# Dense gates of a product-key expert layer: both keys of eight tokens marked in one VectorE comparison, the weighing of four tokens moved to GpSimd

## The reference, cut to what matters

```python
v1, i1 = lax.top_k(s1, PEER_TOPK)
v2, i2 = lax.top_k(s2, PEER_TOPK)
...
top_s, pos = lax.top_k(cand, PEER_TOPK)
eidx = jnp.take_along_axis(cidx, pos, axis=-1)
gates = jax.nn.softmax(top_s, axis=-1)
...
act = jnp.einsum('td,ted->te', xb, u_tab[eb]).astype(jnp.float32)
act = jax.nn.gelu(act, approximate=False) * gb
return jnp.einsum('te,ted->td', act.astype(xb.dtype), v_tab[eb])
```

## Time and profile before

| what | us |
|---|---|
| median of 3 runs | 3903.03 |
| the three runs | 3894.15, 3903.03, 3905.36 |
| the profiled execution's own time | 3899.16 |
| its span, first to last instruction | 3897.4 |
| gate stage, from the first mark to the last copy out of PSUM | 118.8 |

### The profile page before, as it was taken

How to read it: one execution, slowest core, us unless ns; L and a number is a source line. 1 busy time by engine, 2 the same in 40 slices (tenths; PEclk the granted TensorE clock), 3 DMA queues, 4 the chain that set the end, 5 groups by cost and what they waited for, 6 DMA issues and landing times.

```text
span 3897.4 us, 59055 instructions
## 1 busy us (share of the span) xinstructions
PE 3546.3 (91%) x20968; PEld 3128.5 (80%) x20968; DVE 2908.0 (75%) x3762; ACT 1175.3 (30%) x1890; POOL 1160.8 (30%) x986
## 2 busy tenths in 40 slices
PE   7999999999997896994879999999999999999886
PEld 3687787778776683443779999999999999999885
DVE  1555565664665312799879999999999999999987
ACT  1222212322222222113933333333333333333331
POOL 1343444444441544002022222222222222222231
PEclk8999999999998897997989999999999999999998
DMA  9443333333334432112689999999999999999995
GB/s 362 152 128 112 108 119 116 110 116 116 114 111 152 166 111 90 65 65 71 207 310 373 374 366 369 367 371 374 369 367 374 374 368 377 370 362 374 352 350 222
DMA packets 300858, 950.05 MB, mean 244 GB/s; under 512 B 24386, under 2 KB 67842, under 8 KB 230018
## 3 DMA queue, kind: packets, MB, share of 16 engines
q1 hardware_dynamic: 243202, 542.47, 40.1%
q0 software_dynamic: 55296, 402.68, 26.4%
q10 hardware_dynamic: 2304, 4.20, 0.3%
HBM read 914.55 MB, written 33.60 MB: 243 GB/s over the span
## 4 chain that ended last, share of the span: by engine, by line
DVE 16%; DVEq 15%; PE 6%; issue 6%; ACT 4%; DMA 3%; ACTq 0%; SPq 0%; POOLq 0%
DVEq L1987 14%; DVE Ub L1985 6%; ACT UH L1209 3%; DVE acc_r L1993 2%; DVE UL L1213 2%; DMA VR<-peer_v 2%; DVE VL L1949 2%; DVE acc_x L1993 1%; PE PS L1834 1%; PE PS L1835 1%; PE PS L1836 1%; DVE GB L1955 1%; ACT AHa L1896 1%; PE PS L1227 0%; PE PS L1228 0%
## 5 line engine op out<-in xcount | busy, mean ns | idle before, releaser
L1227 PE MATMUL PS<-xh,UH 128*128 128x320 f32 x2048 | 633.3, 309 | 17.6 <-POOL UL L1213 17.6
L1835 PE MATMUL PS<-AL,VH 128*128 128x320 f32 x2048 | 641.4, 313 | 0.0
L1228 PE MATMUL PS<-xl,UH 128*128 128x320 f32 x2048 | 633.6, 309 | 0.0
L1229 PE MATMUL PS<-xh,UL 128*128 128x320 f32 x2048 | 633.4, 309 | 0.0
L375 PE MATMUL PS<-hH,WH 128*128 128x512 f32 (+1 forms) x1312 | 484.0, 369 | 8.3 <-ACT kk L690 7.4
L1787 POOL DMA_INDIRECT Vb<-peer_v,stage x192 | 242.8, 1264 | 772.8 <-DVE acc_r L1993 513.1
L376 PE MATMUL PS<-hL,WH 128*128 128x512 f32 (+1 forms) x1312 | 464.0, 354 | 0.0
L377 PE MATMUL PS<-hH,WL 128*128 128x512 f32 (+1 forms) x1312 | 463.1, 353 | 0.0
L1834 PE MATMUL PS<-AHa,VH 128*128 128x320 f32 x1024 | 325.6, 318 | 110.3 <-DVE AL L1959 81.7
L1227 PEld LDWEIGHTS PS<-xh,UH 128*128 128x128 f32 x2048 | 385.2, 188 | 17.8 <-issue 17.8
L1787 POOL DMA_INDIRECT Ub<-peer_u,stage x192 | 225.3, 1174 | 583.4 <-DVE Ub L1985 535.7
(11 more groups left out here) (331 smaller groups left out, 7284.8 us busy)
## 6 DMA issues: line engine op xcount, KB each, us to landing
UR<-peer_ut SPq DMA_DIRECT2D x128, 1024.0 KB, 7.0
VR<-peer_v SPq DMA_DIRECT2D x256, 512.0 KB, 8.0
AW<-wada SPq DMA_DIRECT2D x128, 512.0 KB, 3.8
WR<-wseq SPq DMA_DIRECT2D x224, 256.0 KB, 2.6
wr<-wada SPq DMA_DIRECT2D x32, 1024.0 KB, 11.3
gates_dram<-GS SPq DMA_DIRECT2D x10, 2048.0 KB, 8.9
GB<-gates_dram SPq DMA_DIRECT2D x32, 640.0 KB, 6.4
oR<-wout SPq DMA_DIRECT2D x32, 512.0 KB, 3.8
```

Of the source, the lines that this page charges most:

```text
L1227: pe.matmul(dst, UH[:, j % 2, k, :], xh[:, k, :], start=(k == 0), stop=False)
L1228: pe.matmul(dst, UH[:, j % 2, k, :], xl[:, k, :], start=False, stop=False)
L1229: last = pe.matmul(dst, UL[:, j % 2, k, :], xh[:, k, :], start=False, stop=(k == KT - 1))
L1835: pe.matmul(low, VH[:, slot, j, cols], AL[:, :, b, :], start=False, stop=False)
```

## The change

- `GACT` goes from 6 to 4: ScalarE weighs the last four tokens of a unit, no longer six.
- `W1` and `O2` become two halves of one buffer `marked`, so that VectorE marks the first and the second keys of all eight tokens in one comparison of 128x2048, with one semaphore behind it. The two instructions that compared and weighed in one are gone.
- GpSimd, after `u_low` of the first four blocks, weighs the first four tokens of each unit in place: four `tensor_scalar` multiplications of 128x128, after waiting for the mark. TensorE waits for these in place of `s_w1`. The fifth `u_low` stands behind all 160 of them in GpSimd's order.

(A short description that came with the change speaks of three tokens on GpSimd and five on ScalarE; the diff sets four and four, and that is what is built.)

```diff
-GACT = 6
+GACT = 4
...
-            O2 = over("O2", "lng", [P, GSLOTS, GU, P], skip=ROW // 2)
-            W1 = over("W1", "lng", [P, GSLOTS, GU, P], skip=ROW // 2 + 2 * ROW)
+            marked = over("marked", "lng", [P, GSLOTS, 2, GU, P], skip=ROW // 2)
+            W1, O2 = marked[:, :, 0, :, :], marked[:, :, 1, :, :]
...
-                            pe.wait_ge(s_w1, 8 * r + j + 1)
+                            pe.wait_ge(s_wp, 8 * r + j + 1)
...
-                    for j in range(SUPER + 1):
-                        u_low(pool, j // SUPER, j % SUPER)
+                    for j in range(SUPER):
+                        u_low(pool, 0, j)
+                    for n in range(GUNITS):
+                        pool.wait_ge(s_e1, n + 1)
+                        pool.sem_inc(s_passed)
+                        for i in range(GU - GACT):
+                            w = W1[:, n % GSLOTS, i, :]
+                            last = pool.tensor_scalar(w, w, pairT[:, 2, GU * n + i:GU * n + i + 1], None, ALU.mult)
+                        last.then_inc(s_wp, 1)
+                    u_low(pool, 1, 0)
...
-                            dve.tensor_tensor(W1[:, slot, GU - GACT:GU, :],
-                                              pairT[:, 0, bass.ds(t0 + GU - GACT, GACT)].unsqueeze(2).to_broadcast([P, GACT, P]),
-                                              iota.unsqueeze(1).to_broadcast([P, GACT, P]), ALU.is_equal).then_inc(s_e1, 1)
-                            dve.tensor_tensor(O2[:, slot, :, :], pairT[:, 1, bass.ds(t0, GU)].unsqueeze(2).to_broadcast([P, GU, P]),
-                                              iota.unsqueeze(1).to_broadcast([P, GU, P]), ALU.is_equal)
-                            for i in range(GU - GACT):
-                                tok = bass.ds(t0 + i, 1)
-                                last = dve.tensor_scalar(W1[:, slot, i, :], iota, pairT[:, 0, tok], pairT[:, 2, tok], ALU.is_equal, ALU.mult)
-                            last.then_inc(s_w1, 1)
+                            dve.tensor_tensor(marked[:, slot, :, :, :], pairT[:, 0:2, bass.ds(t0, GU)].unsqueeze(3).to_broadcast([P, 2, GU, P]),
+                                              iota.unsqueeze(1).unsqueeze(1).to_broadcast([P, 2, GU, P]), ALU.is_equal).then_inc(s_e1, 1)
```

More of the change, by code:

```diff
@@ L1169, in program @@
         s_pairs, s_prpe, s_prev = sem("pairs_ready"), sem("pairs_turned"), sem("pairs_turned_kept")
-        s_e1, s_w1, s_wa1 = sem("first_keys_marked"), sem("keys_marked_and_weighted"), sem("first_keys_weighted_act")
+        s_e1, s_wp, s_wa1 = sem("keys_marked"), sem("first_keys_weighted_pool"), sem("first_keys_weighted_act")
         s_gpe, s_gev = sem("gate_tokens_summed"), sem("gate_tokens_kept")
```

## The result

The changed kernel takes 3962.8 us (median of four runs, 3960.95 to 3967.31), against 3900.6 of before on the same chips (with a fourth run beside the three of the table ahead): ratio 1.0159, 95% interval 1.0145 to 1.0172. It is **62 us slower**, three and a half times the 18 us that were forecast, and outside the range. The direction and the mechanism were those of the forecast; the price of a weighing was not.

What follows compares the result with a forecast made beforehand. ScalarE was taken to bound the gate stage (118.8 us) at 2.66 us a unit. With the change 40 x 3.23 = 129.2, plus 4.6, 1.0 and 2, total 137: +18 us, 3921 us, range 3904 to 3950.

Steps and rivals of the forecast that it cites:

- What bounds the kernel: Gate stage: ScalarE sets the pace at 2.66 us a unit; what the 118.8 us stage gains or loses, the kernel does.
- The exclusion: VectorE's mark and GpSimd's weighing block each other wholly, so a unit costs their sum, 3.23 us in place of 2.66.
- The rounds: Gate stage: VectorE marks up to four units ahead and stops; GpSimd then finishes units, TensorE getting about three in a bunch.
- I take 0.27 us for each of four in a row, near the select: Price of GpSimd's weighing of 128x128, taken from the select's row: 1.08 us a unit for four.
- 166 plus little: Rival of dearer weighings: 0.5 us each, a unit 4.15 us, +47, 3950 us; chance 0.20 together with slow clock.
- The brief lock: Rival: GpSimd holds the port only 0.11 us a weighing, a unit costs about 2.85 us, +3 to +10; chance 0.16.
- A slow TensorE: Rival: bursts of units lower TensorE's clock, +15 us on top, 3936; chance 0.20 together with dearer weighings.
- No exclusion: Rival: marks leave GpSimd room, VectorE's 2.20 us is the gate stage's pace, -16 us, 3887; chance 0.09.
- What was costed at nothing: Fifth `u_low` (4.5 us at most if uncovered), two `dense_dots` (7 us each), stores, GpSimd's waits and instruction fetch: hidden, 0 us.

Runs made afterwards that it cites:

- the PSUM run: Changed kernel with iota copied once into PSUM, where VectorE's mark reads it; GpSimd still does four weighings a unit: 3889.8 us, ratio to before 0.9970.
- the run with 512 elements: Changed kernel with one GpSimd tensor_scalar of 128x512 per unit, by one token's gate for all four, in place of four multiplications: 3924.0 us, one run.

## Why the prediction was wrong

**What bounds the kernel, and that the stage passes on what it loses: right.** 59.0 of 62 us are the stage, and the wait behind it is unchanged.

**The exclusion: right.** It had been read from two long `u_low`; the PSUM run shows it by taking it away. The mark's share of the sum is 2.0 us, where the forecast had 2.15. The rounds were also as described: VectorE runs ahead, stops at `s_gpe`, and GpSimd then delivers three units in a bunch (two in some later rounds).

**The term that failed: "I take 0.27 us for each of four in a row, near the select".** It measures 0.58 from start to start. Put into the same sum, with 0.44 for the one behind each mark (2.59 less the mark's 2.15), a unit is 2.15 + 0.44 + 3 x 0.58 = 4.33 and 40 of them 173. The profile's 172.1 is that number only because the wait of 3.7 us and the two marks that cost GpSimd nothing nearly cancel. The error is 1.1 us in a unit, 44 us in 40 of them (the end of the stage was 3 us shorter than I had it). And the upper end that I had put on this price, 0.53 by the two-input rate, was itself too low: I had argued that an instruction with one tensor input can't be dearer than one with two. Its price per element, 2.5 ns, is above that of the subtraction's 2.1 and three times the cast's 0.83. The rows showed three kinds of GpSimd instruction and none of this one; for an operation that no row shows, rates of other operations were no bound. With its 0.5 a unit would be 4.15 and the loss some 7 us less than it was; and I had closed that case with "166 plus little", though the forecast's own sum had 8 us for the end.

**The brief lock.** I gave it 0.16, as a way to a small loss. For this instruction the hold on VectorE is indeed brief, and that saved nothing. In the run with 512 elements a mark started at 1864.64 us, 1.0 us into a multiplication of 1.56 us, and was not delayed:

```profile
L1687 DVE TENSOR_TENSOR marked<-pairT,iota x1: 2291/2291/2291, 1864.6 to 1864.6; 128x2048 f32<-128x2048 f32 x1
L1459 POOL TENSOR_SCALAR marked<-marked,pairT x3: 1558/2713/5306, 1860.9 to 1865.2; 128x512 f32<-128x512 f32 x3
```

The rows are the mark and the three multiplications around it, of which the one of 1558 ns ran from 1863.64; the last, from 1865.2 on, waited for the rest of this mark and a whole second one, 5.3 us. The next round repeats it: a mark of 2.29 us from 1874.18, 1.0 us into a multiplication of 1.56. Three units take 9.54 us there, 3.18 each, where 1.56 + 2.01 would be 3.57: for this instruction the two times do not add up wholly, though the prediction had the two engines block each other wholly. I infer that a mark is held up only by the first part of such an instruction, while the weighing behind a mark is held up for nearly all of it: in the changed kernel marks lost 0.1 us and weighings 2.0. Since GpSimd was the pace, it was its loss that counted: 4 x 0.58 + 2.0 = 4.33 again. I had asked how long GpSimd holds VectorE up; the question was which of the two engines has no time to lose.

**A slow TensorE** was seen (clock 0.74 in the window) and can have cost no more than a part of GpSimd's one wait of 3.7 us and of the 3.2 us behind the last weighing; I had it at 15 us.

**No exclusion: -16 us.** As a case it was wrong, as a price it was good: the runs that remove the exclusion or the weighing came out 10 to 14 under before.

**What was costed at nothing.** The fifth `u_low` stayed so: it ran from 2006.60 to 2011.1 us, beside the last store. `dense_dots` did not. Their cover was to be four units, 13 us; when the first group began, at 1909.55 us, GpSimd had work only until 1918.63, and the next mark was ready at 1922.15. That is the wait of 3.7 us; with cheaper weighings it grew, to 9.4 with three tokens on GpSimd and 6.8 with one multiplication.

## What to carry to other kernels

Before work goes to idle GpSimd, look at what VectorE runs at that time: if it has two inputs in SBUF and GpSimd reads, reckon that their times add, and moving one of VectorE's inputs to PSUM takes the exclusion away, here 73 us for three lines added and one changed. Where an operation has no row in the trace, another operation's rate on the same engine is not an upper bound; on GpSimd, time the form itself, and prefer one two-input multiplication with a broadcast to several `tensor_scalar` (1.04 us against 4 x 0.58 for the same 512 elements). And an exclusion that looks symmetric should be charged to the engine that becomes the pace.

## What the runs showed of the hardware that I had not expected

- GpSimd's `tensor_scalar` multiplication in float32: 0.60 us for 128 elements, 1.556 for 512 (2.5 ns an element); with a constant 0.52 for 128. The two-input multiplication with a broadcast operand: 1.04 for 512. A fill of 128: 0.206.
- VectorE's comparison of 2048 elements costs the same whether `iota` lies in SBUF or PSUM, 2.29 and 2.28 us.
- The exclusion is of reads: 160 fills beside marks with two SBUF inputs weren't delayed at all. That a `tensor_scalar` on GpSimd holds VectorE up only in its first part is inferred from when marks could start and from units of 3.18 us where the sum is 3.57; it wasn't measured by itself.
